# A hybrid trunk step on one core: where the mixer's first four weight tiles are kept and when they are loaded, and the place of the gate rows' sum

## The reference, cut to what matters

```python
x = x + 0.5 * swiglu(rms_norm(x, g_ffn1), w_ffn1_gate, w_ffn1_up, w_ffn1_down)
proj = rms_norm(x, g_mix) @ w_in           # (1024 x 4104): q, k, v, o of 4 mLSTM heads, q, k, v, g of 4 retention heads,
                                           # then 4 input-gate and 4 forget-gate columns
ig = i_pre + b_gates[:4]                   # per frame and head
lf = log_sigmoid(f_pre + b_gates[4:])
y  = concat(mlstm(q, k, v, ig, lf), retention(rope(q), rope(k), v)) @ w_out
x = x + y
x = x + 0.5 * swiglu(rms_norm(x, g_ffn2), w_ffn2_gate, w_ffn2_up, w_ffn2_down)
out = rms_norm(x, g_final)
```

## Time and profile before

| | |
|---|---|
| median of 3 runs | 1065.79 us (1063.15 to 1066.21) |
| the profiled execution | 1065.65 us |
| its span in the profile | 1063.9 us |
| TensorE matmul busy | 1039.8 us, 98% of the span |
| TensorE weight load busy | 1031.2 us, 97% |
| VectorE busy | 793.0 us, 75% |
| ScalarE busy | 514.8 us, 48% |
| GpSimd busy | 216.0 us, 20% |
| DMA | 142.13 MB, 134 GB/s in the mean |
| 40 slices of 26.6 us | TensorE at 9 tenths or more in all but slice 15 (5 tenths) and the last (6) |

### The profile page before, as it was taken

One profiled execution on the slowest core, in us unless ns is written; L12 is line 12 of the kernel. 1 busy time (PEld: TensorE's weight loads), 2 busy tenths in 40 slices (PEclk: granted clock), 3 DMA queues, 4 the chain that ended last, 5 costly groups with the idle time before them and its releaser, 6 DMA issues.

```text
span 1063.9 us, 20869 instructions
## 1 busy us (share of the span) xinstructions
PE 1039.8 (98%) x8229; PEld 1031.2 (97%) x8229; DVE 793.0 (75%) x1497; ACT 514.8 (48%) x943; POOL 216.0 (20%) x190
## 2 busy tenths in 40 slices
PE   9999999999999959999999999999999999999996
PEld 8999999999999959999999999999999999999996
DVE  6985688987889856465655556588557889788997
ACT  6453366645666535333332223436326664466654
POOL 1100212122211211021222332210012212221210
PEclk9999999999999989999999999999999999999999
DMA  7536887888787664435444324543767877887762
GB/s 224 128 74 147 192 175 161 168 190 177 163 184 132 120 129 98 86 74 77 80 67 73 80 60 79 122 109 70 189 136 162 176 172 169 179 174 173 165 115 95
DMA packets 217050, 142.13 MB, mean 134 GB/s; under 512 B 8684, under 2 KB 214676, under 8 KB 216824
## 3 DMA queue, kind: packets, MB, share of 16 engines
q1 hardware_dynamic: 160824, 110.98, 40.0%
q0 software_dynamic: 56048, 29.79, 21.8%
q10 hardware_dynamic: 80, 0.02, 0.0%
HBM read 135.80 MB, written 3.29 MB: 131 GB/s over the span
## 4 chain that ended last, share of the span: by engine, by line
PE 88%; DMA 4%; DVE 4%; issue 2%; ACT 1%; SPq 0%; POOL 0%; DVEq 0%
PE dense L877 38%; PE dense L753 34%; PE core_banks L877 6%; PE core_banks L753 3%; DMA w_raw<-in_w_in 2%; PE dense L823 1%; DMA sum_ident<-sq 1%; DVE w_lo L1756 1%; DMA w_raw<-in_w_ffn_down 1%; PE core_banks L1093 1%; PE core_banks L1108 1%; PE core_banks L1111 1%; PE core_banks L1083 1%; DVE h_op L1798 1%; DMA x_tok<-in_x_prompt 1%
## 5 line engine op out<-in xcount | busy, mean ns | idle before, releaser
L1293 ACT ACTIVATE w_hi<-w_src 128x512 fp32r<-128x512 f32 x182 | 113.2, 628 | 98.2 <-PE dense L877 55.8
L753 PE MATMUL dense<-xg_hi,w_hi 128*128 128x272 f32 x672 | 143.1, 294 | 11.3 <-DVE rows L2220 10.9
L1293 ACT ACTIVATE w_hi<-w_raw 128x512 fp32r<-128x512 f32 x182 | 112.4, 629 | 76.5 <-PE dense L877 51.4
L877 PE MATMUL dense<-h_op,w_hi 128*128 128x272 f32 x768 | 148.0, 291 | 0.9 <-DVE h_op L1798 0.9
L1756 DVE TENSOR_TENSOR w_lo<-w_src,w_hi 128x512 fp32r<-128x512 f32 x182 | 124.5, 688 | 29.8 <-ACT w_hi L1293 27.7
L1756 DVE TENSOR_TENSOR w_lo<-w_raw,w_hi 128x512 fp32r<-128x512 f32 x182 | 123.7, 687 | 29.7 <-ACT w_hi L1293 28.1
L753 PE MATMUL dense<-xg_lo,w_hi 128*128 128x272 f32 x672 | 139.5, 289 | 0.0
L753 PE MATMUL dense<-xg_hi,w_lo 128*128 128x272 f32 x672 | 139.3, 288 | 0.0
L877 PE MATMUL dense<-x_late_hi,w_hi 128*128 128x272 f32 x432 | 125.7, 291 | 0.0
L877 PE MATMUL dense<-x_op_hi,w_lo 128*128 128x272 f32 x432 | 124.5, 288 | 0.0
L877 PE MATMUL dense<-x_late_hi,w_lo 128*128 128x272 f32 x432 | 124.5, 288 | 0.0
(11 more groups left out here) (363 smaller groups left out, 2389.7 us busy)
## 6 DMA issues: line engine op xcount, KB each, us to landing
w_raw<-in_w_ffn_up SPq DMA_DIRECT2D x43, 512.0 KB, 4.8
w_src<-in_w_ffn_gate SPq DMA_DIRECT2D x36, 512.0 KB, 5.1
w_raw<-in_w_in SPq DMA_DIRECT2D x32, 512.0 KB, 8.6
w_src<-in_w_ffn_gate POOLq DMA_DIRECT2D x36, 256.0 KB, 5.5
w_raw<-in_w_ffn_up POOLq DMA_DIRECT2D x36, 256.0 KB, 5.5
w_src<-in_w_ffn_down SPq DMA_DIRECT2D x16, 512.0 KB, 5.5
w_raw<-in_w_ffn_down SPq DMA_DIRECT2D x16, 512.0 KB, 5.5
w_raw<-in_w_ffn_down SPq DMA_DIRECT2D x16, 384.0 KB, 6.0
```

Source lines behind the costliest of these rows:

```text
L753: last = nc.tensor.matmul(out[:, half, 0:TH], w[:, s % 4, k, :], x(kt)[:, half * TH:(half + 1) * TH], start=start and n == 0 and m == 0, s ...
L877: last = nc.tensor.matmul(out, w[:, k, :], x, start=o in OPENS and k == 0 and m == 0, stop=k == KH - 1 and m == 2, skip_group_check=o not ...
L1293: nc.scalar.activation(block_of(w_hi, n, o), source(e, o), ACT.Copy).then_inc(block_hi, 1)
```

## The change

It does four things. (1) T1 gets a buffer of its own, in_first, and is loaded in FFN 1, right behind the weights of the first two steps. (2) The quarters of odd steps lie in slots 2, 0 and 3 of w_raw, and slot 1 is free of them. Loads into the four slots wait for other numbers of blocks (RAW_READ: 5 for slot 2, 6 for slot 3, all 7 for slot 0, none for slot 1), for D1 to D4 as well as for T2, T3 and T4; T3 is no longer loaded ahead of the last step's quarters, and T5, which goes into slot 1, has no wait. (3) VectorE copies the lower half of the gate product (36 rows, from row 64) to SBUF and adds the upper half to it, ahead of the reciprocal; this frees the banks. The multiplications by rstd come after it, two in place of four, each with an addition of the bias, the forget row first, and ScalarE waits for the first alone. (4) GpSimd's constants wait until w_lo of T1 is made, since they share memory with in_first. Three small buffers are merged into one, which only renames them.

```diff
-        eps = sb("eps", [P, 1])
-        unused = sb("unused", [P, 1])
-        row_small = sb("row_small", [H, 16])
+        smalls = sb("smalls", [P, 16])
+        row_small, eps, unused = smalls[0:H, 0:12], smalls[:, 12:13], smalls[:, 13:14]
...
+        RAW_OF = (2, 0, 3)
+        RAW_READ = {2: 5, 3: BLOCKS - 1, 0: BLOCKS}
+        in_first = sb("in_first", [P, DT, P])
...
+        gate_copy = weights[0:32 + H, :]
...
-            part = w_raw[:, a // 2, KH * (a % 2):KH * (a % 2 + slots), :] if e else w_src[:, a:a + slots, :, :]
+            part = w_raw[:, RAW_OF[a // 2], KH * (a % 2):KH * (a % 2 + slots), :] if e else w_src[:, a:a + slots, :, :]
...
+        def unit_raw(s):
+
+            return in_first[:, :, :] if s == U_IN else w_raw[:, s % RAW, 0:k_tiles(s), :]
...
-                if s in (U_IN, U_IN + 1, U_IN + 3):
-                    sp.wait_ge(block_lo, BLOCKS * STEP_LAST + (2, BLOCKS, 6)[s % RAW])
-                elif s >= RAW:
+                if U_IN < s < U_IN + RAW:
+                    sp.wait_ge(block_lo, BLOCKS * STEP_LAST + RAW_READ[s % RAW])
+                elif s >= RAW and s != U_IN + RAW:
                     sp.wait_ge(w_lo_ready, s - RAW + 1 + step * i)
...
-                if j < RAW:
-                    sp.wait_ge(block_lo, BLOCKS * (STEPS * n + STEP_DOWN) + (2, BLOCKS, 6, 6)[s % RAW])
+                if j < RAW and s % RAW in RAW_READ:
+                    sp.wait_ge(block_lo, BLOCKS * (STEPS * n + STEP_DOWN) + RAW_READ[s % RAW])
...
                 for p in PAIRS[0]:
                     load_pair(p)
+                if n == 0:
+                    sp.dma_start(in_first[:, :, :], w_rows(w_in)[:, :, 0:P]).then_inc(in_loaded, 16)
...
-                        if step_of_down(n, c, d) == STEP_LAST:
-                            load_in(0, 2)
...
-                    if h or u != 2:
+                    if h or u:
                         load_in(h, u)
...
-            def gate_rows_start():
+            def take_gates():
+
                 dve.wait_ge(unit_done, U_GATE + 1)
                 tile = halves(bank_of(T_GATE))
-                nc.vector.tensor_tensor(split_cols(rows[:, I_ROW, :]), tile[0:H], split_cols(rstd[0:H, :]), ALU.mult)
-                nc.vector.tensor_tensor(split_cols(rows[:, F_ROW, :]), tile[32:32 + H], split_cols(rstd[32:32 + H, :]), ALU.mult)
-                nc.vector.tensor_tensor(split_cols(rows[:, E_ROW, :]), tile[64:64 + H], split_cols(rstd[64:64 + H, :]), ALU.mult)
-                nc.vector.tensor_tensor(split_cols(rows[:, LF_ROW, :]), tile[96:96 + H], split_cols(rstd[96:96 + H, :]), ALU.mult)\
-                    .then_inc(evicted, 1)
+                nc.vector.tensor_copy(split_cols(gate_copy), tile[64:96 + H]).then_inc(gates_copied, 1)
+                dve.wait_ge(gates_copied, 1)
+                nc.vector.tensor_tensor(split_cols(gate_copy), tile[0:32 + H], split_cols(gate_copy), ALU.add).then_inc(evicted, 1)
+
+            def gate_rows_start():
+
                 dve.wait_ge(evicted, T_GATE + 1)
                 dve.wait_ge(gates_loaded, 16 * 4)
-                nc.vector.scalar_tensor_tensor(rows[:, I_ROW, :], rows[:, I_ROW, :], row_small[:, 0:1], rows[:, E_ROW, :],
-                                               ALU.add, ALU.add)
-                nc.vector.scalar_tensor_tensor(rows[:, F_ROW, :], rows[:, F_ROW, :], row_small[:, 1:2], rows[:, LF_ROW, :],
-                                               ALU.add, ALU.add).then_inc(gates_biased, 1)
+                for a, row in ((1, F_ROW), (0, I_ROW)):
+                    part = slice(32 * a, 32 * a + H)
+                    link(nc.vector.tensor_tensor(rows[:, row, :], gate_copy[part], rstd[part, :], ALU.mult))
+                    last = nc.vector.tensor_scalar(rows[:, row, :], rows[:, row, :], row_small[:, a:a + 1], None, ALU.add)
+                    last.then_inc(gates_biased, 1)
...
             split_lo(0, U_IN + 1, 0)
+            take_gates()
             invert_root(1)
             gate_rows_start()
...
             pool.wait_ge(product_done, BLOCKS * STEPS)
+            pool.wait_ge(w_lo_ready, U_IN + 1)
```

More of the change, by code:

```diff
@@ L339, in hybrid_trunk_step @@
         at["next"] = max(ffn_end, mixer_end)
+        assert U_IN % RAW == 1 and 1 not in RAW_READ
         assert at["next"] <= nc.sbuf_usable_end, (at["next"], nc.sbuf_usable_end, ffn_end, mixer_end)
@@ L481, in hybrid_trunk_step @@
         gates_loaded = sem("gates_loaded")
+        in_loaded = sem("in_loaded")
         gate_slots_zeroed = sem("gate_slots_zeroed")
@@ L513, in hybrid_trunk_step @@
         gates_biased = sem("gates_biased")
+        gates_copied = sem("gates_copied")
         gates_ln = sem("gates_ln")
@@ L1224, in split_hi @@
                     return
-                loads = len([m for m in range(s % RAW, s + 1, RAW) if m != U_GATE])
-                act.wait_ge(w_loaded[s % RAW], 16 * loads + 16 // RAW * step * i)
-                raw = w_raw[:, s % RAW, 0:k_tiles(s), :]
+                if s == U_IN:
+                    act.wait_ge(in_loaded, 16)
+                else:
+                    loads = len([m for m in range(s % RAW, s + 1, RAW) if m not in (U_GATE, U_IN)])
+                    act.wait_ge(w_loaded[s % RAW], 16 * loads + 16 // RAW * step * i)
+                raw = unit_raw(s)
                 unit = down_unit(s)
@@ L1699, in split_lo @@
                 nk = k_tiles(s)
-                nc.vector.tensor_tensor(w_lo[:, s % 4, 0:nk, :], w_raw[:, s % RAW, 0:nk, :],
+                nc.vector.tensor_tensor(w_lo[:, s % 4, 0:nk, :], unit_raw(s),
                                         w_hi[:, s % 4, 0:nk, :].bitcast(F32), ALU.subtract).then_inc(w_lo_ready, 1)
```

## The result

| | before | changed |
|---|---|---|
| median of the runs | 1066.0 us (4 runs, 1063.15 to 1066.76) | 1047.89 us (4 runs, 1047.59 to 1048.20) |
| the profiled execution, its span | 1065.65, 1063.9 us | 1047.74, 1046.0 us |
| TensorE matmul busy | 1039.8 us, 98% | 1033.6 us, 99% |
| VectorE, ScalarE, GpSimd busy | 793.0, 514.8, 216.0 us | 791.3, 515.1, 215.8 us |

The 1065.79 us given above for the kernel before is the median of three of these four runs. The ratio is 0.9835 (95% interval 0.9817 to 0.9853): 1.65% faster, some 18 us.

The account below looks back on a forecast made before the run. It took TensorE's 10.86 us wait at T2's product as the bound: a late load, root and reciprocal, and reading of banks in series. 1065.65 - 12.6 (entry) + 1.2 (FFN 1) - 1.2 (FFN 2) = 1053.05 us; range 1051.3 to 1057.8.

Parts of the forecast that it names:

- three small buffers are merged: Buffers allocated together in the change; taken as a renaming, with no term in the sum.
- T3's landing: Entry to the mixer: T3's load lands at 386.5, so gate_columns starts at 398.3, 1.0 us after TensorE is there.
- its rule: Entry to the mixer: gate_columns can start 11.8 us after T3's load lands.
- nothing waits: Rival, entry and FFN: T3 lands by 385.5, fills disturb nothing, FFN 1 loses only 0.5; 1051.5 us, chance 0.15.
- TensorE's own arrival: Entry to the mixer: T1's product starts at 380.5; without a gap TensorE reaches gate_columns 16.8 us later, at 397.3.
- The 10.86 us of idling and the slow stretch: TensorE at T2's product: the idling goes, and the half-clock stretch behind it, worth 1.7 us.
- The gates' chain: VectorE at the mixer's entry: copy and addition take 1.45 us together, end at 382.7; forget row ready about 387.4.
- The fills: GpSimd's mixer constants, moved later: may stretch VectorE's gate work, 0 to 0.5 us showing; chance 0.07 that it is seen.
- The down tiles: Waits before the first down products: +1.2 us in FFN 1 (bounds 0.5 to 1.4), -1.2 in FFN 2 (0 to 1.22).
- T1's load: Moved some 300 us ahead in FFN 1, into a gap of the DMA engines before D1; costed at nothing.
- The prediction's terms for the entry: Entry to the mixer: 0.4 + 0.44 + 10.86 + 1.7 is 13.4, less 1.0; 12.6 us used.

Follow-up runs that it names:

- the transposes: Kernel before with 60 transposes of a constant put ahead of T2's product, in TensorE's idling: 1062.04 us, ratio 0.9969.
- the repeat: The changed kernel, unaltered, run again beside the version with slots in the order 0, 3, 2: 1047.98 us, ratio 0.983.
- the other slots: Changed kernel with the quarters of odd steps in slots 0, 3, 2 instead of 2, 0, 3: 1046.64 us, then 1046.69 us side by side.
- the run with T3 late: Changed kernel with T3 loaded behind T4 and the table: 1058.66 us, ratio 0.9933.
- the loads without the gates' order: Changed kernel, merged buffers included, with the old gate-row code behind the reciprocal: 1049.25 us, ratio 0.9866.

## Why the prediction was wrong, point by point

- **The failed step: "three small buffers are merged", costed at nothing.** It moved the operands of every product by 64 bytes, and 3.3 us of the 5.2 missed come from it. Done alone, and done by an inserted gap in its place, it turns the same 12.05 into 11.95 us. It had no term in the sum and no rival. The measured time plus 3.3 is 1051.2 us, still at the edge of the range (1051.3): to come near the forecast, T3's landing and FFN 1 had to be right too.
- **T3's landing was mis-sized.** Predicted 386.5 (bounds 385.8 to 388.8), measured 381.2. The mechanism was right: with T3 at 393.0 the wait came as its rule says. At 381.2 it is not the last, and the 1.0 us does not appear; the rival "nothing waits", given 0.15, is what happened, except that its 1051.5 us is 3.6 too high, by the same missing 3.3. Instead the gate chain hangs on the forget row, ready at 387.1, and leads from there to gate rows at 396.2. I took 9.8 us as the bound for T3's gap to T2, and it was 10.1, but T2 landed at 371, not 376: the first load took 7.9 us and not 12.5. This is not chance: in the six profiles where the first of these loads is issued between 362.7 and 363.9 us it took 7.9 to 10.5 us, in the eight where it is issued between 365.3 and 369.4 it took 12.3 to 12.8. What slows the later ones isn't shown.
- **TensorE's own arrival** at gate_columns was predicted at 397.3 and was 396.8: T1's product began at 380.4 (380.5), and 66 pairs took 16.44 us (16.8). The faster products are 0.14 of the difference; the rest is the 0.254 us per pair, read behind the slow stretch, where the undisturbed pieces of the kernel before give 12.05 / 48 = 0.251.
- **The 10.86 us of idling and the slow stretch** went as forecast; the clock's 1.7 us agree with the 1.6 of the transposes.
- **The gates' chain** was right: copy and addition took 0.73 and 0.72 (1.45 forecast for both), the forget row was ready at 387.1 (387.4).
- **The fills** cost VectorE nothing where they now run: split_lo of T2 takes 1.22 us beside them, 1.23 before without them. GpSimd's own first selection on the mask takes 0.81 us there, 0.29 before. That they had stretched the addition at 377.22 is borne out by all profiles: 1.16 us in the seven with the fills beside it, 0.72 in the seven with the fills later. The addition behind it, at 378.48, took 0.72 beside the small fills even before, so it was the selection (1.22 us from 376.58) or the fill that followed it that did it.
- **The down tiles.** FFN 2 gained the 1.2, but only half of the profiles with the old load order have this wait, so that the profiled execution had it is luck; the change takes away a wait that comes and goes. FFN 1 lost 0.6 here and 0.9 in the repeat (forecast 1.2, bounds 0.5 to 1.4).
- **T1's load** was hidden, as forecast: in_first landed 13.9 us after its issue at 50.85, ahead of D1.

The prediction's terms for the entry add up to 13.4 - 1.0 = 12.4 us, not quite the 12.6 that it used.

By sum, between the forecast of 1053.05 and the profiled 1047.74: 1.0 for T3, 0.75 for the rest of the entry (14.35 against 12.6 us in all; 0.4 of it ahead of T1's product and 0.3 in the 66 pairs), 0.6 in FFN 1 and 3.8 for the rows "little by little" make 6.15; the start and the end of the program, where nothing was changed, took back 0.85. That leaves 5.3. Of the 3.8, 3.3 are counted by the pieces of 96; the last 0.5 is not traced to an operation.

## What to carry to other kernels

An edit that changes the size of any buffer moves all buffers behind it: where one engine is busy for 99% of the time, compare the length of an undisturbed piece of its work before and after, and try a few paddings by themselves. A load that is issued too early is not free either, since it slows a small transfer that other work waits for; here a start 1.4 us after that transfer's left it nearly alone (3.6 us against 3.3). And where a slot's wait decides when a load starts, give the slot that is read first to the tile that is needed first.

## What the runs showed of the hardware

- The same 96 matmuls of 128 x 272 took 12.05, 12.00 or 12.11, 11.95 and 12.03 us with their moving operands 32, 64, 96 and 0 bytes behind a multiple of 128, in every profile of each kind.
- GpSimd's addition of squares (272 KB) took 3.3 us alone, 3.6 us with T2 issued 1.4 us behind it (the other slots), 8.9 us with T2 to T4 issued with it (9.1 in the repeat) and 11.8 us in the run with T3 late. At 8.9 us it cost TensorE nothing, at 9.5 us (the loads without the gates' order) T1's product began 0.6 us later, and at 11.8 us TensorE waited 2.5 us.
- An addition of two 128 x 544 tensors on VectorE took 1.16 us beside GpSimd's selection and fill in seven profiles, 0.72 us in the seven with GpSimd idle beside it.
- A load of w_in (512 KB) landed between 5.5 and 21.1 us after its issue in one execution of the changed kernel, 8.4 us in the median. The first of the loads at the entry landed after 7.9 to 10.5 us when issued by 363.9 us and after 12.3 to 12.8 when issued from 365.3 on. Landing times are the least certain term of such a sum, and bounds from a single row are too narrow.
